# Adding a mixture-of-experts block's rows to the output in 4 KB pieces instead of 1 KB pieces

## The reference

```python
logits = (ht @ router_w) + router_b
top_val, top_idx = lax.top_k(logits, 4)          # 4 of 32 experts per token
gates = jax.nn.softmax(top_val, axis=-1)
# per expert, on its own tokens
gu = xb @ w_gu + b_gu                            # 1024 -> 2048
gate = jnp.minimum(gu[:, :D_FF], 7.0); up = jnp.clip(gu[:, D_FF:], -7.0, 7.0)
act = (up + 1.0) * (gate * jax.nn.sigmoid(gate * 1.702))
yb = act @ w_down + b_down                       # 1024 -> 1024
y = jnp.zeros((T, D)).at[row_token].add(yb * row_gate[:, None])
```

## Time and profile before

| what | us |
|---|---|
| median of 3 runs (1324.72 to 1338.38) | 1324.82 |
| the profiled execution's own time | 1326.72 |
| span of its trace | 1324.8 |
| TensorE busy | 1188.7 (90%) |
| VectorE busy | 530.7 (40%) |
| GpSimd busy | 276.4 (21%) |
| ScalarE busy | 215.2 (16%) |
| mean granted TensorE clock | 0.976 of full |

### The profile page before, as it was taken

One profiled execution on the slowest core, in us unless ns is written; L12 is line 12 of the kernel. 1 busy time (PEld: TensorE's weight loads), 2 busy tenths in 40 slices (PEclk: granted clock), 3 DMA queues, 4 the chain that ended last, 5 costly groups with the idle time before them and its releaser, 6 DMA issues.

```text
span 1324.8 us, 30781 instructions
## 1 busy us (share of the span) xinstructions
PE 1188.7 (90%) x12045; PEld 551.5 (42%) x12046; DVE 530.7 (40%) x1333; ACT 215.2 (16%) x450; POOL 276.4 (21%) x372
## 2 busy tenths in 40 slices
PE   7999999998899889889888889899998987988895
PEld 6875556855333333333233333333333332333332
DVE  2337856557333333333333333343343332333332
ACT  3136664321100000000000000000000000000000
POOL 1000012000122222222222222232221221222222
PEclk9999999999999999999999999999999987999998
DMA  5132145088899999999999999999999999999994
GB/s 189 51 106 64 32 127 146 21 350 348 361 413 416 418 418 417 418 418 415 416 419 416 382 373 405 390 396 405 402 417 417 418 421 420 416 417 420 418 417 168
DMA packets 67649, 446.43 MB, mean 337 GB/s; under 512 B 16992, under 2 KB 37672, under 8 KB 43040
## 3 DMA queue, kind: packets, MB, share of 16 engines
q1 hardware_dynamic: 48736, 424.97, 77.6%
q0 software_dynamic: 16128, 18.78, 6.2%
q10 hardware_dynamic: 2752, 2.23, 0.5%
HBM read 435.24 MB, written 15.07 MB: 340 GB/s over the span
## 4 chain that ended last, share of the span: by engine, by line
DMA 62%; PE 23%; issue 6%; ACT 4%; DVE 3%; POOLq 1%; ACTq 0%; POOL 0%; SPq 0%; DVEq 0%
DMA out<-Y,IDXS 55%; PE PS L690 16%; DMA W<-in_expert_w_gate_up 4%; ACT Y L679 3%; PE PS L1099 3%; DMA XG<-hn_scratch,IDXC 2%; PE PSC L690 2%; PE PS L1114 1%; POOLq L443 0%; DMA W<-in_norm_mix_w 0%; PE PS L866 0%; PE PS L700 0%; DVE W L1165 0%; DVE W L1338 0%; DVE W L1337 0%
## 5 line engine op out<-in xcount | busy, mean ns | idle before, releaser
L1099 PE MATMUL PS<-W,XT 128*32 128x512 f32 x5184 | 600.3, 615 | 108.5 <-DVE XT L1517 90.3
L1099 PEld LDWEIGHTS PS<-W,XT 128*32 128x32 f32 x5184 | 167.8, 112 | 498.3 <-issue 405.2
L1114 PE MATMUL PS<-W,AT 128*32 128x256 f32 x5184 | 295.2, 379 | 2.7 <-DVE SIG L1545 2.2
L690 PE MATMUL PS<-W 128*128 128x512 f32 (+6 forms) x874 | 244.2, 437 | 2.1 <-ACT W L618 1.1
L1114 PEld LDWEIGHTS PS<-W,AT 128*32 128x32 f32 x5184 | 171.1, 110 | 146.9 <-issue 48.5
L1522 DVE TENSOR_TENSOR GU<-PS,BGU 128x512 f32<-128x512 f32 x81 | 56.0, 691 | 362.6 <-PE PS L1099 362.6
L690 PEld LDWEIGHTS PS<-W 128*128 128x128 f32 (+1 forms) x874 | 145.4, 190 | 81.9 <-issue 71.4
L679 ACT ACTIVATE Y<-SIG,ident 128x256 f32<-128x256 f32 x81 | 41.2, 508 | 812.3 <-DMA out<-Y,IDXS 801.4
L434 POOL DMA_INDIRECT out<-Y,IDXS x81 | 130.5, 1611 | 102.8 <-ACT Y L679 95.9
L1517 DVE STREAM_TRANSPOSE XT<-XG 128x256 f32<-128x256 f32 x81 | 52.0, 642 | 189.3 <-DMA XG<-hn_scratch,IDXC 189.3
L430 POOL COPY IDXS<-IDX 128x1 uint32 (+1 forms) x81 | 15.0, 185 | 493.1 <-DMA out<-Y,IDXS 493.1
(11 more groups left out here) (281 smaller groups left out, 523.7 us busy)
## 6 DMA issues: line engine op xcount, KB each, us to landing
W<-in_expert_w_gate_up SPq DMA_DIRECT2D x128, 2048.0 KB, 24.2
W<-in_expert_w_down SPq DMA_DIRECT2D x64, 2048.0 KB, 24.8
W<-in_w_in SPq DMA_DIRECT2D x10, 1024.0 KB, 5.5
W<-in_x SPq DMA_DIRECT2D x8, 512.0 KB, 11.1
W<-in_w_out SPq DMA_DIRECT2D x2, 1024.0 KB, 9.8
W<-in_w_out SPq DMA_DIRECT2D x1, 2048.0 KB, 8.0
hn_scratch<-W POOLq DMA_DIRECT2D x4, 512.0 KB, 11.9
out<-W ACTq DMA_DIRECT2D x4, 512.0 KB, 11.5
```

The lines of the kernel that those rows point to most:

```text
L690: return pe.matmul(o, l, r, start=st, stop=sp_)
L1099: last = pe.matmul(GPS[32 * j:32 * j + 32, :].rearrange("p (g n) -> p g n", g=2), XT[:, 32 * k:32 * k + 32], rhs, start=(k == 0), stop=(k ...
L1114: last = pe.matmul(DPS[32 * j:32 * j + 32, :], AT[:, 32 * k:32 * k + 32], DNW[p][:, k, j * QW:(j + 1) * QW], start=(k == 0), stop=(k == KD ...
```

## The change

The change does five things.

1. The scatter: ACT writes a block's Y as 32 partitions by 1024 (four activations, each moving 32 partitions to partitions 0 to 31), and POOL's scatter adds 32 rows of 4 KB to the output, by token numbers in a new table `IDXT` (`IDX` shifted right by 2). Y grows from 1 KB to 4 KB per partition.
2. The list tables move from W1's last 16 KB to W0 from column 22272, and to BGU, AT, BDN, SIG and Y, which are idle then. W1's second down part can be loaded once the output projection is through; W0's second down part now waits for the second `lists_done`.
3. `gate_lists` runs behind the last k of the first block instead of behind k = 4.
4. Expert 0's further blocks are one loop on PE instead of a branch and a loop.
5. `HNT` is one buffer of its own, and the descriptor scratch is 8192 bytes.

```diff
-        Y = sb("Y", QW)
+        Y = sb("Y", D)
...
+        HNT = sb("HNT", D)[:, :].rearrange("p (k n) -> p k n", k=KD)
...
-        LISTS = W1[:, 20480:24576]
+        LISTS = W0[:, 22272:24080]
...
+        EQ = BGU[1][:, :].rearrange("p (t k m) -> p t k m", t=NT, k=TOPK)
+        TG = [v.rearrange("p (t k m) -> p t k m", t=2, k=TOPK) for v in (AT[:, :], BDN[1][:, :])]
+        T1 = [v.rearrange("p (k m) -> p k m", k=TOPK) for v in (SIG[:, 0:P], SIG[:, P:2 * P], Y[:, 0:P], Y[:, P:2 * P])]
...
             gu_part(1, 1, [0])
+            dn_part(1, 1, [1])
             sp.wait_ge(S_("hn_ready"), NT)
...
             gu_part(1, 1, [1])
+            sp.wait_ge(S_("lists_done"), 1)
+            sp.wait_ge(S_("gathered"), 16)
+            sp.wait_ge(S_("lists_done"), 2)
+            dn_part(0, 0, [1])
             gu_bias(1, 1)
             dn_bias(1, 1)
-            sp.wait_ge(S_("lists_done"), 1)
-            sp.wait_ge(S_("gathered"), 16)
-            dn_part(0, 0, [1])
-            sp.wait_ge(S_("lists_done"), 2)
-            dn_part(1, 1, [1])
...
-                g.tensor_copy(IDXS[:, :], IDX[:, bass.ds(at, 1)]).then_inc(S_("idx_scat"), 1)
+                g.tensor_copy(IDXS[0:BT, :], IDXT[0:BT, bass.ds(at, 1)]).then_inc(S_("idx_scat"), 1)
...
-                g.indirect_dma_start(out=acc_d, out_offset=bass.IndirectOffsetOnAxis(ap=IDXS[:, :], axis=0),
-                                     in_=Y[:, :], in_offset=None, compute_op=ALU.add,
-                                     bounds_check=ROWS - 1, oob_is_err=False).then_inc(S_("scattered"), 16)
+                g.indirect_dma_start(out=out, out_offset=bass.IndirectOffsetOnAxis(ap=IDXS[0:BT, :], axis=0),
+                                     in_=Y[0:BT, :], in_offset=None, compute_op=ALU.add,
+                                     bounds_check=S - 1, oob_is_err=False).then_inc(S_("scattered"), 16)
...
-                    if t >= 2:
-                        a.wait_ge(S_("lg_ps"), t - 1)
-                    a.activation(HNT[t % 2][:, 4 * half:4 * half + 4, :], h4(PS[2 + half]), ACT.Copy).then_inc(S_("ht_ready"), 1)
+                    if t >= 1:
+                        a.wait_ge(S_("lg_ps"), t)
+                    a.activation(HNT[:, 4 * half:4 * half + 4, :], h4(PS[2 + half]), ACT.Copy).then_inc(S_("ht_ready"), 1)
...
-                a.activation(Y[:, :], SIG[:, :], ACT.Copy, scale=GATEB[:, bass.ds(at, 1)]).then_inc(S_("ys_ready"), 1)
+                for j in range(4):
+                    js = slice(BT * j, BT * j + BT)
+                    ins = a.activation(Y[0:BT, QW * j:QW * j + QW], SIG[js, :], ACT.Copy, scale=GATEB[js, bass.ds(at, 1)])
+                ins.then_inc(S_("ys_ready"), 1)
...
-            between = {1: token_lists, 2: token_table, 4: gate_lists}
+            between = {1: token_lists, 2: token_table, KD - 1: gate_lists}
...
             with pe.If(last > 0):
-                gate_up(1, 0, 16, False, False)
-                down(0, 0, 16)
-            with pe.If(last > 1):
-                with pe.Fori(2, last + 1) as i:
+                with pe.Fori(1, last + 1) as i:
                     gate_up(i, 0, 16, False, False)
                     down(i - 1, 0, 16)
...
+            v.wait_ge(S_("lists_done"), 1)
+            ts(IDXT[0:BT, :], IDX[0:BT, :], 2, None, ALU.logical_shift_right).then_inc(S_("rows_done"), 1)
+            for half in range(2):
+                ts2 = slice(2 * half, 2 * half + 2)
+                tt(TG[half], EQ[:, ts2], GATE[:, 8 * half:8 * half + 8].rearrange("p (t k m) -> p t k m", t=2, m=1).to_broadcast([P, 2, TOPK, BT]),
+                   ALU.mult).then_inc(S_("tg_ready"), 1)
...
+                if first:
+                    v.wait_ge(S_("gate_ps"), 1)
                 v.wait_ge(S_("d_ps"), i + 1)
...
-    nc = _bacc.Bacc("TRN2", target_bir_lowering=False, num_devices=1)
+    nc = _bacc.Bacc("TRN2", target_bir_lowering=False, num_devices=1, dynamic_dma_scratch_size=8192)
```

More of the change, by code:

```diff
@@ L47, in S_ @@
             return sems[name]
-        acc_d = out.rearrange("t (j n) -> (t j) n", j=4)
         hn_d = nc.dram_tensor("hn_scratch", (ROWS, QW), F32).ap()
@@ L63, in hybrid_block @@
         IDX = sb("IDX", MAXB + 1, U32)
+        IDXT = sb("IDXT", MAXB + 1, U32)
         IDXC = sb("IDXC", 2, U32)
@@ L137, in hybrid_block @@
         SQK = [B[c]["KAT"] for c in range(NT)]
-        HNT = [W1[:, 20480 + D * i:20480 + D * i + D].rearrange("p (k n) -> p k n", k=KD) for i in range(2)]
         HN = [W1[:, 4096 + D * t:4096 + D * t + D] for t in range(NT)]
@@ L172, in hybrid_block @@
         BASE = RT[:, 1620:1748].rearrange("p (t e) -> p t e", t=NT)
-        LISTS = W1[:, 20480:24576]
+        LISTS = W0[:, 22272:24080]
         OHB = LISTS[:, 0:512].rearrange("p (t k e) -> p t k e", t=NT, k=TOPK)
         B1 = LISTS[:, 0:NT * TOPK * (MAXB + 1)].rearrange("p (t k b) -> p t k b", t=NT, k=TOPK)
-        EQ, T1, TG = [LISTS[:, 1552 + 512 * i:2064 + 512 * i].rearrange("p (t k m) -> p t k m", t=NT, k=TOPK) for i in range(3)]
-        L4, G4 = [LISTS[0:MAXB + 1, 3088 + P * i:3216 + P * i] for i in range(2)]
+        EQ = BGU[1][:, :].rearrange("p (t k m) -> p t k m", t=NT, k=TOPK)
+        TG = [v.rearrange("p (t k m) -> p t k m", t=2, k=TOPK) for v in (AT[:, :], BDN[1][:, :])]
+        T1 = [v.rearrange("p (k m) -> p k m", k=TOPK) for v in (SIG[:, 0:P], SIG[:, P:2 * P], Y[:, 0:P], Y[:, P:2 * P])]
+        L4, G4 = [LISTS[0:MAXB + 1, 1552 + P * i:1680 + P * i] for i in range(2)]
         GATEB = ident[:, 0:MAXB + 1]
@@ L441, in _ @@
             next_gather(3)
+            g.wait_ge(S_("rows_done"), 1)
             scatter(0)
@@ L1018, in logits @@
                 for k in range(KD):
-                    last = mm(LGP[t % 2], HNT[t % 2][:, k, :], RW[:, k, :], k == 0, k == KD - 1)
+                    last = mm(LGP[t % 2], HNT[:, k, :], RW[:, k, :], k == 0, k == KD - 1)
                 last.then_inc(S_("lg_ps"), 1)
@@ L1076, in token_lists @@
                     for k in range(TOPK):
-                        last = mm(PS[4][0:MAXB + 1, 0:BT], B1[:, t, k, :], T1[:, t, k, :], t == 0 and k == 0, t == NT - 1 and k == TOPK - 1)
+                        last = mm(PS[4][0:MAXB + 1, 0:BT], B1[:, t, k, :], T1[t][:, k, :], t == 0 and k == 0, t == NT - 1 and k == TOPK - 1)
                 last.then_inc(S_("list_ps"), 1)
@@ L1083, in gate_lists @@
             def gate_lists():
-                pe.wait_ge(S_("tg_ready"), 1)
+                pe.wait_ge(S_("tg_ready"), 2)
                 for i in range(4 * TOPK):
                     t, k = i // TOPK, i % TOPK
-                    last = mm(PS[5][0:MAXB + 1, 0:BT], B1[:, t, k, :], TG[:, t, k, :], i == 0, i == 4 * TOPK - 1)
+                    last = mm(PS[5][0:MAXB + 1, 0:BT], B1[:, t, k, :], TG[t // 2][:, t % 2, k, :], i == 0, i == 4 * TOPK - 1)
                 last.then_inc(S_("gate_ps"), 1)
-            between = {1: token_lists, 2: token_table, 4: gate_lists}
+            between = {1: token_lists, 2: token_table, KD - 1: gate_lists}
             def gate_up(i, p, rnd, first_of_expert, first):
@@ L1493, in _ @@
             for t in range(NT):
-                ts(T1[:, t], EQ[:, t], TOKM[:, t:t + 1], None, ALU.mult).then_inc(S_("t1_ready"), 1)
+                ts(T1[t], EQ[:, t], TOKM[:, t:t + 1], None, ALU.mult).then_inc(S_("t1_ready"), 1)
                 blocks_of(t)
@@ L1512, in _ @@
             stt(out=IDX[:, :], in0=LISTP, scalar=PJ, in1=LPAD, op0=ALU.add, op1=ALU.add).then_inc(S_("lists_done"), 1)
-            tt(TG, EQ, GATE[:, :].rearrange("p (t k m) -> p t k m", t=NT, m=1).to_broadcast([P, NT, TOPK, BT]), ALU.mult).then_inc(S_("tg_ready"), 1)
+            v.wait_ge(S_("lists_done"), 1)
[4 more added lines that the diff above has]
+                   ALU.mult).then_inc(S_("tg_ready"), 1)
             v.wait_ge(S_("lists_done"), 1)
```

## The result

| | median us | range, runs | ratio to before, 95% |
|---|---|---|---|
| before | 1326.45 | 1324.72 to 1338.38, 13 | |
| changed | 1316.37 | 1314.92 to 1319.40, 13 | 0.9924 [0.9909, 0.9940] |

A forecast was written before the change was run, and what follows sets the result against it. The prediction took full DMA engines as the bound, with time lost only where weights are asked for too late; -7.6 - 12 - 6 - 1.6 - 1 = -28.2 us gave 1297 us, range over all cases 1283 to 1322.

The forecast's parts named there:

- Packets: Scatter: 2048 adding packets of 4 KB at 0.32 us replace 8192 of 1 KB at 0.095 us, -7.6 us per engine.
- addition costs a fixed 0.055 us: Scatter packets, one bound: an adding 4 KB packet takes only 0.205 us, -22.4 us instead of -7.6.
- rival three: Scatter: addition costs more per KB, 0.45 us a packet, so +9 us instead of -7.6, 1313 us; chance 8%.
- Latency and pace: Scatter loop: about 7.1 us from issue to landing instead of 10.84, blocks every 10.3 us instead of 12.3.
- What the pace is worth in 750 to 970: Stretch 750 to 970 us: the faster loop takes back 12 of 13 us of idle DMA time, -12 us.
- Rival one: Scatter: the 32 rows don't reach all 16 engines; with eight carrying the additions +12.7 us, 1338 us; chance 12%.
- The tail, -6: End of the weight loads: the last parts are no longer asked for late, -6 of 7 us.
- Start, -1.6: Start of expert phase: 5 us of earlier W1 load fill the 310 to 340 hole, later W0 costs 3.4; sum -1.6.
- End, -1: Last scatter: it lands about 2 us earlier, four activations cost 1.5 us more, issue is a bit shorter; -1 us.
- Rival two: Block loop: gather or fixed latency holds blocks at 11 us or more, idle stretches stay; -10.2 us, 1315 us; chance 18%.

The follow-up runs named there:

- a_plain: The changed kernel with the scatter writing its rows without addition; measured 1299.97 us, ratio 0.9831.
- a_mix2: The changed kernel with each block's tokens placed in a mixed order that gives engines 0 to 3 a little less; measured 1304.69 us, ratio 0.9832.
- b_scat: The kernel before with only the scatter changed (32 rows of 4 KB, four activations, the table and smaller descriptor scratch they need); measured 1319.69 us, ratio 0.9941.
- b_mix: The kernel before with each block's tokens spread over its places in a mixed order; measured 1317.32 us, ratio 0.9948.

## Why the prediction was wrong, by its own steps

**Packets: right.** 0.32 us was taken for an adding 4 KB, 0.327 was measured (0.319 of the engine's time). A window of the steady stretch, 682 to 684 us, has 36 packets of the software queue with 0.12 MB, which are 29 of 4 KB and 7 small ones. They take 0.299 x 2 x 16 / 29 = 0.33 us each if the small ones cost nothing:

```profile
q1 hardware_dynamic: 40, 0.62, 74.0%
q0 software_dynamic: 36, 0.12, 29.9%
```

The queue's share fell from 6.2% to 5.4%; 5.6% was forecast. One reading was off: the 102 packets of the earlier trace rows hold 0.10 MB, so some 95 of them are of 1 KB and the rest small ones. An adding KB then lasts 0.101 us and not 0.095, and by the durations the packets' difference is (8192 x 0.101 - 2048 x 0.327) / 16 = 9.9 us an engine, some of which is overlap. The finding that the queues take turns stands, with 95 beside 92 of 16 KB. The bound "addition costs a fixed 0.055 us" is excluded by a_plain's packets, and rival three's 0.45 us as well.

**Latency and pace: right.** 7.5 us to land for 7.1, 10.3 us a block for 10.3. The gather is off the path. TensorE waits for weights by 130 us where some 100 were named.

**What the pace is worth in 750 to 970: right in its window, wrong in the sum.** "I take back 12 of the 13 us: -12" came true as a mean over engines. The failed step is to enter it as time at the end. It treats sixteen engines as one pipe, and adds the mean of the packets' cost to the mean of the idle time. The step's own ground, "a full resource can't be sped up by asking it earlier", holds for each engine by itself: before, at a mean share of 0.98, the fullest engine was idle for about 2 of those 13 us, by the moments with hardly a packet in flight. The rest was won by light engines, which by theory A had to wait for the fullest one again at 1154 us and at the end. What the runs show of it without the theory is that idle time of the mean in 750 to 970 shrank by 12.2 us and D by 9.9, that 8.6 us of idle time came back at the two places, and that both shrink when only the order of the tokens changes. Rival one of the prediction even has the sentence that decides ("a weight part is complete only with its slowest engine"), and used it only for the case that half the engines carry nothing.

**The tail, -6: wrong in sign.** Its 7 us were put down to late asking. SP had asked for all 28 us before, as it now does 34 us before. The falling ladder of shares, 0.61, 0.52, 0.38, was the picture of uneven engines, and the earlier trace rows gave it as one number, 0.43. By D's balance the tail's idle time grew by 5.2 us to 10.9; in a_mix2 it is some 3 us.

**Start, -1.6: small, right in sign.** The row of the second down part, which was expected at 338, of the reload, and of the matmuls that read the part, answering to the earlier trace rows:

```profile
338.62 0.33 SPq L231 DMA_DIRECT2D W<-in_expert_w_down  x1
...
342.55 4.28 SPq L225 DMA_DIRECT2D W<-in_expert_w_gate_up  x4
...
346.10 3.66 PE L1120 MATMUL PS<-W,AT 128*32 128x256 f32 x64
```

304 instead of 278 GB/s from 310 to 340; but the reload comes 2 us later than before, and 1.2 us of idle time behind 340 are new.

**End, -1: nothing.** From D to the span's end 13.9 us before, 14.0 now. The four activations take 2.06 us for 0.51, and that probably ate the shorter landing; no run separates the two.

**The rivals.** Rival two's 1315 is the measured number, but not for its reason: the pace did not stay. Rival one's mechanism, a row's fixed engine, fits the runs in a milder form: all 16 engines take part, and the loads on them are uneven by the tokens. The range of 1283 to 1322 held the time because it reached over rivals two and three, not because of the mechanism; the forecast missed by 19 us.

What stays open: a_plain's missing 5 us, b_scat's 3, the exact share of each engine, which no trace names, and with it whether the bias loads cost 3 or 5 us. The time behind D is also open: it is 14 us in the kernel before and the changed one, and up to 17 in runs that don't touch it.

## What to carry to other kernels

A DMA share is a mean over sixteen engines: before counting its idle part as time that can be won, look at the last microseconds of the load at 2 to 4 us each. If all was asked for long before and the share falls in steps (0.6, 0.4, 0.25) to the last landing, suspect uneven engines; then only work taken off the fullest one counts. Lists that always leave their last rows empty, and small loads of a few rows, may load the same engines each time. Spreading the rows tests it and costs a table.

## What the runs showed of the hardware

- An adding packet costs twice a plain one of its size: 0.327 against 0.160 us at 4 KB, and 0.101 at 1 KB, so four of 1 KB cost 0.40.
- Which row a token stands in is worth 11.7 us of 1316 with the same bytes and instructions (a_mix2), which fits a row's place in a transfer setting its DMA engine.
- A share of 1.00 or 1.01 over hundreds of us doesn't show that engines are evenly used: it was 1.01 in the changed kernel from 340 to 970 us, and the difference appeared only later, at 1154 us and above all at the end, as 0.25 for 8 us.
- Bias loads of four rows each, 0.4 MB in all, moved the last weight's landing by 3.3 us (away from the fullest engines) to 5.0 us (left out).
- A fall of the granted clock to 0.80 for 50 us, ahead of the weights, put all their loads 10.7 us back (b_mix's profiled execution).
